# Both weight matrices of the chunk's front loaded anew per chunk, and rings of 12 u and 12 v rows in a PEER layer

## What is computed

```
h   = x + concat(RMSNorm(SBAttn(q,k,v)), ConformerConv(c)) @ w_out     [q|k|v|c] = RMSNorm(x) @ w_in
hn  = RMSNorm(h)
qh  = hn @ peer_wq                       # 8 heads x 128
v1,i1 = top16(qh[:, :64] @ k1.T); v2,i2 = top16(qh[:, 64:] @ k2.T)
experts, top_s = top16 of the 16 x 16 sums v1 + v2;  gates = softmax(top_s)
act = gelu(sum_d u_tab[experts] * hn)    # 128 experts per token
out = h + sum over experts of (gates * act) * v_tab[experts]
```

## Time and profile before

| | us |
|---|---|
| timed runs, median of 3 (lowest, highest) | 3090.54 (3089.73, 3090.81) |
| span of the profiled execution, first to last instruction | 3482.5 |
| PE, DVE, POOL, ACT busy in it | 2791.4, 2152.2, 1999.2, 875.1 |
| DMA queue q0 (the gathers), share of 16 engines | 82.6% |

### The profile page before, as it was taken

The page is one execution under the profiler, slowest core; times in us unless marked ns, Lnnn a source line. Parts: engine busy times, 40 slices in busy tenths (PEclk is TensorE's granted clock), DMA queues, the critical chain, the costliest instruction groups (busy, mean ns, idle before and its releaser), DMA issues.

```text
span 3482.5 us, 30095 instructions
## 1 busy us (share of the span) xinstructions
PE 2791.4 (80%) x7609; PEld 1257.9 (36%) x7609; DVE 2152.2 (62%) x5205; ACT 875.1 (25%) x2053; POOL 1999.2 (57%) x2062
## 2 busy tenths in 40 slices
PE   8999488677887888687977888789877988677777
PEld 4445234233432334233432434234432444222222
DVE  1245966865677657756587567856676646744443
ACT  2331221123212331134112421135212532111111
POOL 1000466666666666666667556666666666766665
PEclk9999699999999999999999899999999999999999
DMA  6111799999999999999999889989999998999998
GB/s 216 33 31 67 262 361 343 347 363 370 346 347 352 373 350 328 357 358 364 344 359 357 326 335 331 362 339 342 359 339 358 338 350 321 348 377 359 369 356 343
DMA packets 320463, 1121.47 MB, mean 322 GB/s; under 512 B 36465, under 2 KB 44681, under 8 KB 320296
## 3 DMA queue, kind: packets, MB, share of 16 engines
q0 software_dynamic: 294912, 1073.87, 82.6%
q1 hardware_dynamic: 25384, 45.72, 3.8%
HBM read 1111.01 MB, written 8.45 MB: 321 GB/s over the span
## 4 chain that ended last, share of the span: by engine, by line
PE 24%; issue 20%; DVE 16%; another core or an unknown queue 10%; DMA 9%; POOL 8%; ACT 3%; POOLq 0%; DVEq 0%; ACTq 0%; SPq 0%
PE psum L1433 16%; DVE ring_u L1744 6%; DMA ring_v<-in_peer_v,experts 5%; POOL ring_v L1334 5%; DMA ring_u<-in_peer_u,experts 4%; POOL ring_u L1334 3%; PE psum L949 2%; PE psum L970 1%; PE psum L1391 1%; PE psum L1365 1%; PE psum L1381 1%; DVE acc L1700 1%; DVE top_i L1081 1%; DVE relu_z L1084 1%
## 5 line engine op out<-in xcount | busy, mean ns | idle before, releaser
L1433 PE MATMUL psum<-ring_v,diag 128*128 128x512 f32 x4076 | 2031.7, 628 | 454.2 <-DMA ring_v<-in_peer_v,experts 305.3
L1744 DVE CUSTOM_DVE_ANT_0 ring_u<-ring_u,psum 128x1024 f32<-128x1024 f32 x1024 | 1237.6, 1219 | 564.5 <-DMA ring_u<-in_peer_u,experts 469.9
L1334 POOL DMA_INDIRECT ring_u<-in_peer_u,experts x1024 | 990.9, 968 | 893.9 <-issue 623.3
L1334 POOL DMA_INDIRECT ring_v<-in_peer_v,experts x1024 | 997.5, 974 | 577.4 <-issue 279.1
L1433 PEld LDWEIGHTS psum<-ring_v,diag 128*128 128x128 f32 x4076 | 744.2, 198 | 1498.2 <-issue 1372.2
L1577 ACT ACTIVATE diag<-ident,weights 128x128 f32<-128x128 f32 x1019 | 360.1, 392 | 966.8 <-issue 348.3
L483 PE MATMUL psum<-w_sb,xnT 128*128 128x512 f32 x560 | 246.6, 599 | 0.0
L1700 DVE SCALAR_TENSOR_TENSOR acc<-conv_in,taps,acc 128x128 f32<-128x128 f32 x840 | 239.5, 348 | 9.4 <-remote 8.6
L1669 DVE TENSOR_TENSOR_SCAN log_keep<-log_keep,relu_z 128x256 f32<-128x256 f32 (+3 forms) x88 | 90.5, 1028 | 173.2 <-ACT log_keep L1510 86.9
L970 PEld LDWEIGHTS psum<-actT,w_kept 128*128 128x128 f32 x1024 | 136.8, 199 | 75.1 <-issue 75.1
L970 PE MATMUL psum<-actT,w_kept 128*128 128x128 f32 x1024 | 139.4, 282 | 21.3 <-issue 21.1
(11 more groups left out here) (188 smaller groups left out, 1570.5 us busy)
## 6 DMA issues: line engine op xcount, KB each, us to landing
ring_u<-in_peer_u,experts POOLq DMA_INDIRECT x1024
ring_v<-in_peer_v,experts POOLq DMA_INDIRECT x1024
w_sb<-in_w_in SPq DMA_DIRECT2D x4, 2048.0 KB, 19.6
x_in<-in_x SPq DMA_DIRECT2D x8, 512.0 KB, 4.4
w_kept<-in_w_out SPq DMA_DIRECT2D x1, 4096.0 KB, 13.6
h_res<-in_x SPq DMA_DIRECT2D x8, 512.0 KB
w_kept<-in_peer_wq SPq DMA_DIRECT2D x1, 4096.0 KB, 14.1
wo_sb<-in_w_out SPq DMA_DIRECT2D x1, 4096.0 KB, 12.7
```

The lines of the kernel that those rows point to most:

```text
L1334: nc.gpsimd.indirect_dma_start(ring[kind][:, at, :], None, peer_u[0] if kind == "u" else peer_v[0], bass.IndirectOffsetOnAxis(S.experts[c ...
L1433: last = nc.tensor.matmul(y_ps[:, j * BANK:(j + 1) * BANK], diag[:, e % DIAGS, :], ring["v"][:, n % RING["v"], j * BANK:(j + 1) * BANK], s ...
L1744: nc.vector.tensor_tensor_reduce(out=row, in0=row, in1=hn, scale=1.0, scalar=0.0, op0=ALU.mult, op1=ALU.add, accum_out=dots[:, e:e + 1]).t ...
```

## The change

`wo_sb` goes (32 KB per partition) and `w_kept` is used by phase0 alone; in phase1 its 32 KB are eight of the 24 ring slots. A ring of 12 u rows and one of 12 v rows are made of 16 new slots and those eight. For each chunk from 1 on both matrices are loaded again, through four buffers of 4 KB that the front has done with: `relu_z[0]`, `relu_z[1]`, `attT`, and `log_keep[1]` for w_out or `log_keep[0]` for peer_wq. w_out comes as eight tiles of 128 rows by 1024 columns; peer_wq as four tiles of 256 rows by 512 columns, for the first four heads and then for the last four. So `mix` and `query` go over the weight's row tiles outside and the outputs inside. SP issues these 16 loads of 512 KB, each when its buffer is free; PE waits for each tile. SP's order changes: the next chunk's q and convolution input now come ahead of the chunk's weights.

```diff
-RING = {"u": 5, "v": 7}
+RING = {"u": 12, "v": 12}
+BUFS = 4
...
+def wo_landed(f, k):
+    loads = 2 if k % BUFS == BUFS - 1 else 4
+    return 16 * (loads * (f - 1) + k // BUFS + 1)
+def wq_landed(f, buf, half):
+    before = 0 if buf == BUFS - 1 else 2
+    return 16 * ((2 + before) * (f - 1) + before + half + 1)
+def wo_read(f, k):
+    return (KT_D + BUFS - 2) * (f - 1) + k + 1
+def wq_read(f, buf):
+    return wo_read(f, KT_D - 2) + buf + 1
...
-    wo_sb = late.tile("wo_sb", [P, KT_D, D], F32)
...
+    S.wo_bufs = (relu_z[0][:, :], relu_z[1][:, :], attT[:, :, :].rearrange("p b t -> p (b t)"), log_keep[1][:, :])
+    S.wq_bufs = [b.rearrange("p (k n) -> p k n", n=BANK) for b in
+                 (relu_z[0][:, :], relu_z[1][:, :], attT[:, :, :].rearrange("p b t -> p (b t)"), log_keep[0][:, :])]
...
-            sp.wait_ge(projected[V], CHUNKS)
-            sp.dma_start(wo_sb[:, :, :], w_out[0].rearrange("(k p) n -> p k n", p=P)).then_inc(S.wo_loaded, 16)
...
         for m in range(total * n // MIX_SLOTS, total * (n + 1) // MIX_SLOTS):
-            j, k = m // KT_D, m % KT_D
...
+            k, j = m // 2, m % 2
+            if not later(f):
+                weight = wo_sb[:, k, j * BANK:(j + 1) * BANK]
+            else:
+                if j == 0:
+                    pe.wait_ge(S.wo_in[k % BUFS], wo_landed(f, k))
+                weight = S.wo_bufs[k % BUFS][:, j * BANK:(j + 1) * BANK]
...
+            elif later(f) and j == 1:
+                product.then_inc(S.weight_read, 1)
...
         for m in range(total * n // QUERY_SLOTS, total * (n + 1) // QUERY_SLOTS):
-            h, k = m // KT_D, m % KT_D
...
+            half, k, h = m // (heads * KT_D), m // heads % KT_D, m % heads
+            buf, kept = k // 2, k % 2
+            if later(f):
+                if kept == 0 and h == 0:
+                    pe.wait_ge(S.wq_in[buf], wq_landed(f, buf, half))
+                weight = S.wq_bufs[buf][:, kept, h * P:(h + 1) * P]
...
-    ring = {kind: m.tile(f"ring_{kind}", [P, RING[kind], D], F32) for kind in "uv"}
+    fresh = m.tile("ring", [P, RING["u"] + RING["v"] - KT_D, D], F32)
+    slots = [fresh[:, n, :] for n in range(RING["u"] + RING["v"] - KT_D)] + [w_kept[:, n, :] for n in range(KT_D)]
+    ring = {"u": slots[:RING["u"]], "v": slots[RING["u"]:]}
...
+            def load_mix_weights(f):
+                for k in range(KT_D):
+                    if k >= BUFS:
+                        sp.wait_ge(S.weight_read, wo_read(f, k - BUFS))
+                    elif k < 2:
+                        sp.wait_ge(S.att_T, UNITS * f + 2 * (HEADS - 1 + k))
+                    elif k == 2:
+                        sp.wait_ge(S.attended, HEADS * (f + 1))
+                    else:
+                        sp.wait_ge(S.stick, UNITS * (f + 1))
+                    sp.dma_start(S.wo_bufs[k % BUFS], w_out[0, k * P:(k + 1) * P, :]).then_inc(S.wo_in[k % BUFS], 16)
+            def load_query_weights(f):
+                for half in range(2):
+                    for b in range(BUFS):
+                        if half and b == BUFS - 1:
+                            sp.wait_ge(S.queried, 2 * f + 1)
+                        elif half:
+                            sp.wait_ge(S.weight_read, wq_read(f, b))
+                        elif b < BUFS - 1:
+                            sp.wait_ge(S.weight_read, wo_read(f, BUFS + b))
+                        else:
+                            sp.wait_ge(S.o_T, f + 1)
+                        sp.dma_start(S.wq_bufs[b],
+                                     peer_wq[0, 2 * b * P:2 * (b + 1) * P, half * BANK:(half + 1) * BANK]
+                                     .rearrange("(k p) n -> p k n", p=P)).then_inc(S.wq_in[b], 16)
...
             def step(c, f):
+                if c is None:
+                    load_front(1)
+                    return
                 if f is not None:
-                    load_front(f)
-                if c is not None and later(c):
+                    load_x(f)
+                if later(c):
                     store(c - 1)
+                if f is not None:
+                    if f + 1 < CHUNKS:
+                        load_front(f + 1)
+                    load_mix_weights(f)
+                    load_query_weights(f)
```

More of the change, by code:

```diff
@@ L190, in build @@
     S.c_in = nc.alloc_semaphore("c_in")
-    S.wo_loaded = nc.alloc_semaphore("wo_loaded")
     S.tapped = nc.alloc_semaphore("tapped")
@@ L261, in build @@
     S.dve_passed = nc.alloc_semaphore("dve_passed")
-    phase0(nc, S, keep.at, psum, ident, ident_b, mask, kT, vals, keys_bd, w_kept, wo_sb, actT, qT,
+    phase0(nc, S, keep.at, psum, ident, ident_b, mask, kT, vals, keys_bd, w_kept, actT, qT,
            conv_in, acc, vec, iota16, taps, g_mix, g_attn, b_conv, g_ln, b_ln, g_q, g_k, qT_spill,
@@ L266, in build, with phase0 @@
            conv_ln_b, w_out, norm_ffn_g, peer_wq, peer_k1, peer_k2)
-    phase1(nc, S, late.at, psum, ident, ident_b, mask, kT, vals, keys_bd, w_kept, wo_sb, actT, qT,
+    phase1(nc, S, late.at, psum, ident, ident_b, mask, kT, vals, keys_bd, w_kept, actT, qT,
            conv_in, acc, iota16, taps, g_attn, b_conv, g_ln, b_ln, qT_spill, hT_spill, x,
-           w_out, peer_u, peer_v, out)
-def phase0(nc, S, base, psum, ident, ident_b, mask, kT, vals, keys_bd, w_kept, wo_sb, actT, qT,
+           w_out, peer_wq, peer_u, peer_v, out)
+def phase0(nc, S, base, psum, ident, ident_b, mask, kT, vals, keys_bd, w_kept, actT, qT,
            conv_in, acc, vec, iota16, taps, g_mix, g_attn, b_conv, g_ln, b_ln, g_q, g_k, qT_spill,
@@ L403, in _ @@
             sp.wait_ge(S.mixed, 1)
-            sp.dma_start(w_kept[:, :, :], peer_wq[0].rearrange("(k p) n -> p k n", p=P)).then_inc(S.wq_loaded, 16)
+            sp.dma_start(w_kept[:, :, :], peer_wq[0].rearrange("(k p) n -> p k n", p=P)).then_inc(S.kept_loaded, 16)
             store_q(PENULT)
@@ L944, in mix @@
             pe.wait_ge(S.swished, CB * (f + 1))
-            pe.wait_ge(S.wo_loaded, 32 if later(f) else 16)
+            if not later(f):
+                pe.wait_ge(S.kept_loaded, 16)
         total = 2 * KT_D
         for m in range(total * n // MIX_SLOTS, total * (n + 1) // MIX_SLOTS):
-            j, k = m // KT_D, m % KT_D
-            product = nc.tensor.matmul(z[0][:, j * BANK:(j + 1) * BANK], S.actT[:, k, :],
-                                       wo_sb[:, k, j * BANK:(j + 1) * BANK], start=k == 0, stop=k == KT_D - 1)
+            k, j = m // 2, m % 2
+            if not later(f):
+                weight = wo_sb[:, k, j * BANK:(j + 1) * BANK]
[3 more added lines that the diff above has]
+                weight = S.wo_bufs[k % BUFS][:, j * BANK:(j + 1) * BANK]
+            product = nc.tensor.matmul(z[0][:, j * BANK:(j + 1) * BANK], S.actT[:, k, :], weight,
+                                       start=k == 0, stop=k == KT_D - 1)
             if m == total - 1:
                 product.then_inc(S.mixed, 1)
+            elif later(f) and j == 1:
+                product.then_inc(S.weight_read, 1)
     def transpose_h(f):
@@ L965, in query @@
             pe.wait_ge(S.h_done, f + 1)
-            pe.wait_ge(S.wq_loaded, 16)
+            if not later(f):
+                pe.wait_ge(S.kept_loaded, 32)
+        heads = PH // 2
         total = PH * KT_D
         for m in range(total * n // QUERY_SLOTS, total * (n + 1) // QUERY_SLOTS):
-            h, k = m // KT_D, m % KT_D
-            product = nc.tensor.matmul(z[0][:, h * P:(h + 1) * P], wq_sb[:, k, h * P:(h + 1) * P],
-                                       S.actT[:, k, :], start=k == 0, stop=k == KT_D - 1)
+            half, k, h = m // (heads * KT_D), m // heads % KT_D, m % heads
[5 more added lines that the diff above has]
+            else:
+                weight = wq_sb[:, k, (half * heads + h) * P:(half * heads + h + 1) * P]
+            product = nc.tensor.matmul(z[0][:, (half * heads + h) * P:(half * heads + h + 1) * P], weight,
+                                       S.actT[:, k, :], start=k == 0 and h == 0,
+                                       stop=k == KT_D - 1 and h == heads - 1)
             if m in (total // 2 - 1, total - 1):
                 product.then_inc(S.queried, 1)
+            elif later(f) and half == 0 and kept == 1 and h == heads - 1:
+                product.then_inc(S.weight_read, 1)
     def score_keys(f, pair):
@@ L1207, in vector_front, with phase1 @@
             split_positions, look_up, (match, pick, collect), number_experts, finish_gates)
-def phase1(nc, S, base, psum, ident, ident_b, mask, kT, vals, keys_bd, w_kept, wo_sb, actT, qT,
+def phase1(nc, S, base, psum, ident, ident_b, mask, kT, vals, keys_bd, w_kept, actT, qT,
            conv_in, acc, iota16, taps, g_attn, b_conv, g_ln, b_ln, qT_spill, hT_spill, x,
-           w_out, peer_u, peer_v, out):
+           w_out, peer_wq, peer_u, peer_v, out):
     m = Map(nc, base)
-    ring = {kind: m.tile(f"ring_{kind}", [P, RING[kind], D], F32) for kind in "uv"}
```

(12 more changed lines are left out.)

18 lines of the change are left out of this document (15 added, 3 removed).

## The result

The changed kernel takes 3214.64 us (median of 4, 3213.96 to 3217.56), the kernel before 3090.14 beside it: ratio 1.0405, 95% interval 1.0392 to 1.0417, 124.5 us slower. Forecast were 3218 us and a range from 3155 to 3262.

The account below looks back on a forecast made before the run. The prediction took the DMA engines, full with gathered rows in the second part, to bound the kernel. It summed 3090.5 + 147.5 (weights reloaded) - 20 (bigger rings) + 0 (waits) = 3218 us, range 3155 to 3262.

Parts of the forecast that it names:

- The plateau as the bound: Second part: the 16 DMA engines are already full with five and seven slots, at 406 to 417 GB/s in undisturbed windows.
- Bytes: Chunks 1 to 7 reload w_out and peer_wq, 58.7 MB, hidden by nothing: 71.6 plus 75.9, sum 147.5 us.
- The load removed: wo_sb's 4 MB load ended before the first gather, so dropping it is worth 0, at most 12.7 us.
- PE, DVE and POOL work: Mixing and query products keep number and form, only their order changes: 0 us, between -3 and +5.
- The rings: Five more v and seven more u rows under way win 20 us, between 0 and 70.
- The bound of 70: Most the bigger rings can win: the time the engines are not full, 3,020 us being 70 under the median.
- the 3,020: Old kernel at undisturbed pace: 1,085 MB at 410 GB/s, 365 us ahead, some 8 us behind the last row's landing.
- Added waits: PE's waits for each weight tile at mix and query, mostly covered by 14.0 us: 0 us.
- B: Rival: weight loads queue behind up to 24 gathers and come late at mix and query; about 3300 us, chance 0.07.
- A: Rival: gathers are below the engines' limit, bigger rings reach 417 GB/s, 3,116 us (at 435, 3,002); chance 0.07.
- C: Rival: the rings win nothing and the bytes cost 147.5 us, 3238 us, up to 3286; chance 0.24.
- The span of the profile: Profiled span: 3482.5 plus 168 us for the bytes, less 20 to 50 for the rings, about 3615.

Follow-up runs that it names:

- the square: Four runs, rings 5 and 7 or 12 and 12: without second-part weight loads 3091.2 and 3068.2 us, with all loads 3237.1 and 3214.6 us.
- no_loads_5_7: The changed kernel without weight loads in the second part (mixing and queries read kT) and with the old rings of 5 u and 7 v rows: 3091.23 us.
- no_loads: The changed kernel, rings of 12 and 12, without weight loads in the second part; mixing and queries of chunks 1 to 7 read kT: 3068.15 us.
- loads_5_7: The changed kernel with its weight loads, but with the old rings of 5 u and 7 v rows: 3237.08 us.

## Why the prediction was right

*The plateau as the bound.* Right. With undisturbed windows at 406 to 417 GB/s and small rings, I took the DMA engines for full; the square shows it from both sides, and the quiet profiles stay near 409 in most slices.

*Bytes.* 147.5 us forecast, 146.5 and 145.9 measured; the halves 71.6 and 75.9 forecast, 71.6 and 74.9 measured. That nothing hides them was the step that decided the sign.

*The load removed, PE, DVE and POOL work, the new order.* 0 forecast; no_loads_5_7 differs from before by 0.04%.

*The rings.* 20 us taken out of 0 to 70, measured 22.4 and 23.1. The prediction doesn't derive the 20 inside its bounds, so that the forecast came within 3.4 us of the time is in part luck. What it did work out, at most 15.3 us of work shifted at the start, is what the traces show there, 15; it didn't say that this alone would be two thirds of the gain. The bound of 70 was right but loose: no_loads is still 48 us above the 3,020 that the plateau gives. Against 410 GB/s it lacks 9 us in the first 80 us, where DVE is still late with 12 slots (289 GB/s at 385 to 405), 18 us in the middle at 407, and 22 us in the last 60 us, of which the 3,020 held 8: some 41 of the 48.

*Added waits.* 0 forecast. Tiles landed in 7.1 to 10.1 us in the median against 14.0 of cover, and B did not occur: a load of SP's queue overtakes the 24 gathers (27.3 us). That is what the Trainium skill's rule of going round the queues packet by packet says (DMA: Bandwidth & Descriptors, section Queues, rings and completion order).

*Rivals.* A falls: no 10 us of the changed kernel above 414 GB/s, nor near A's other figure of 435, and rings of 12 and 12 without loads win 23 us, not the 115 that 417 GB/s would give (1,085 / 0.417 + 373 = 2,975 us). C (3238) was the nearest, but loads_5_7 lies 22.4 us above the changed kernel and their runs don't overlap (3234.41 lowest, 3217.56 highest).

*What was wrong.* The span of the profile, about 3615 forecast on the old profile's scale, came out as 3211.9: I had treated 350 GB/s as what a profiled execution has, and it was the condition of the chip. The sum survived since it was made on the median with the plateau's rate. The chunks' lengthening (17 to 20 us) was put a little low: 146.5 / 7 = 20.9, and the rings win next to nothing in the middle chunks. From one chunk's first dot product to the next's, chunks 1 to 5 (the first is 0) of the changed kernel take 20.3 to 22.2 us more than those of no_loads_5_7; the last chunk, to the end, takes 1.9 us less. And that the change is slower at all holds for a quiet chip; the prediction read no condition into its sum under which the sign could turn, as the disturbed chips suggest.

## What to carry to other kernels

Before memory is spent on prefetch, look for the highest rate that the profile holds for 10 us or more with the buffers that there are. In this kernel the engines' share was 1 there, each byte added cost its time, and slots won mainly where a consumer was late (some 15 of 23 us, at the start); sharing the 12 slots that were there gave 11.5 us for no memory. Check a profile's span against the timed median first; where they differ by 12%, take durations from the windows that are undisturbed, not from its mean. And time a change of this kind on more than one chip: here the byte count decided on the quiet ones and did not on the disturbed ones.

## Unexpected

The latency of a gathered row follows the ring's depth: 10.3 us from issue to landing for a u row in loads_5_7, 27.3 with 12 and 12 slots, at the same 409 GB/s. More than ten of the 27.3 us are one engine's lag behind the other fifteen. And the mean DMA share can fall to 0.72 while rows keep landing every 1.26 us, because one engine is behind; here a share under 1 near the end was no room at all.
